# A routed encoder layer on one core: token columns of four experts made together, branches moved ahead of the gate product, a further round's products ahead of the down products

## The reference, cut to what matters

```python
# TOK = 512 tokens (two requests of 256), D = 1024, 32 experts of width 512, top 2 of 8 in the top group of 4
h = (LN(x) * (1 + scale1) + shift1)
t = token_mixer(h)                        # large dense products, done by 431 us
x = LN(alpha * x + gate1 * t)
h = (LN(x) * (1 + scale2) + shift2)
logit_g, logit_e = h @ w_router_group, h @ w_router_expert
top_logit, top_idx = top_k(logit_e of the token's best group, 2)
gate = softmax(logit_g)[g_sel] * softmax(top_logit)
for each expert e:                        # xb: the tokens that chose e
    y = (silu(xb @ w_exp_gate[e]) * (xb @ w_exp_up[e])) @ w_exp_down[e]
f = sum over a token's two experts of gate * y
x = LN(alpha * x + gate2 * f)
```

## Time and profile before

| | |
|---|---|
| median of 3 runs | 959.8 us |
| the profiled execution | 961.72 us, its span 959.9 us |
| TensorE (PE) busy | 913.3 us, 95% |
| VectorE (DVE), ScalarE (ACT), GpSimd (POOL) busy | 382.2, 244.7, 113.2 us |
| chain that ended last, by engine | PE 84%, DVE 4%, ACT 3%, issue 3%, DMA 2% |
| read from and written to HBM | 275.81 and 23.09 MB |

### The profile page before, as it was taken

The page is one execution under the profiler, slowest core; times in us unless marked ns, Lnnn a source line. Parts: engine busy times, 40 slices in busy tenths (PEclk is TensorE's granted clock), DMA queues, the critical chain, the costliest instruction groups (busy, mean ns, idle before and its releaser), DMA issues.

```text
span 959.9 us, 11508 instructions
## 1 busy us (share of the span) xinstructions
PE 913.3 (95%) x4269; PEld 538.9 (56%) x4269; DVE 382.2 (40%) x666; ACT 244.7 (25%) x357; POOL 113.2 (12%) x142
## 2 busy tenths in 40 slices
PE   3999999999999999999999999999898999999994
PEld 2567766888888888786444444434444444444331
DVE  4533443565344236788532223213222222232235
ACT  2422234432233235445411011101100110111024
POOL 2210366000001000000000000000000000000031
PEclk9999999999999999999999999999999999999997
DMA  9985654265565623809999999999999799999974
GB/s 369 348 281 175 252 220 175 88 235 202 206 233 152 178 96 120 267 0 417 375 384 427 425 426 428 426 427 427 426 429 425 315 426 426 428 427 427 423 269 136
DMA packets 47509, 295.51 MB, mean 308 GB/s; under 512 B 5046, under 2 KB 7190, under 8 KB 32082
## 3 DMA queue, kind: packets, MB, share of 16 engines
q1 hardware_dynamic: 37216, 263.99, 68.1%
q0 software_dynamic: 9616, 29.02, 9.1%
q10 hardware_dynamic: 610, 1.66, 0.5%
HBM read 275.81 MB, written 23.09 MB: 311 GB/s over the span
## 4 chain that ended last, share of the span: by engine, by line
PE 84%; DVE 4%; ACT 3%; issue 3%; DMA 2%; SPq 2%; POOL 0%; DVEq 0%; POOLq 0%; ACTq 0%
PE bank L609 81%; PE bank L893 2%; SPq L382 2%; ACT x_rows L1123 2%; DMA modraw<-in_w_mod 1%; DMA y_first<-round_y,pos_y 1%; PE bank L674 0%; DVE wo_lo L1693 0%; DMA round_y<-yout,store_row 0%; DVE y_second L2100 0%; DVE y_second L2113 0%; ACT w_hi L1123 0%; POOL y_second L597 0%; DVE bank L2108 0%; DVE yout L1988 0%
## 5 line engine op out<-in xcount | busy, mean ns | idle before, releaser
L609 PE MATMUL bank<-up_w,x_t 128*64 128x512 f32 x512 | 225.0, 592 | 0.0
L609 PE MATMUL bank<-gate_w,x_t 128*64 128x512 f32 x512 | 225.0, 592 | 0.0
L609 PEld LDWEIGHTS bank<-gate_w,x_t 128*64 128x64 f32 x512 | 70.1, 137 | 142.6 <-issue 142.6
L609 PE MATMUL bank<-h_hi,w_hi 128*128 128x512 f32 x320 | 124.8, 390 | 0.3 <-ACT h_hi L1157 0.3
L609 PE MATMUL bank<-down_w,hid_t 128*64 128x512 f32 x512 | 117.1, 598 | 8.1 <-issue 7.2
L609 PE MATMUL bank<-h_hi,w_lo 128*128 128x512 f32 x320 | 124.7, 390 | 0.0
L609 PE MATMUL bank<-h_lo,w_hi 128*128 128x512 f32 x320 | 124.5, 397 | 0.0
L1357 ACT ACTIVATE sg_hid<-bank 64x512 f32<-64x512 f32 x33 | 19.5, 592 | 350.7 <-PE bank L609 350.7
L1970 DVE TENSOR_TENSOR sg_hid<-bank,sg_hid 64x512 f32<-64x512 f32 x32 | 22.2, 694 | 201.6 <-ACT sg_hid L1357 201.5
L1528 DVE TENSOR_TENSOR w_lo<-raw,w_hi 128x1024 fp32r<-128x1024 f32 x56 | 68.5, 1225 | 77.2 <-ACT w_hi L1123 77.1
L581 POOL DMA_INDIRECT round_y<-yout,store_row x31 | 31.3, 1009 | 486.5 <-DVE yout L1988 460.2
(11 more groups left out here) (319 smaller groups left out, 1109.7 us busy)
## 6 DMA issues: line engine op xcount, KB each, us to landing
down_w<-in_w_exp_down SPq DMA_DIRECT2D x32, 2048.0 KB, 18.1
gate_w<-in_w_exp_gate SPq DMA_DIRECT2D x30, 2048.0 KB, 15.9
up_w<-in_w_exp_up SPq DMA_DIRECT2D x30, 2048.0 KB, 20.8
modraw<-in_w_mod SPq DMA_DIRECT2D x24, 1024.0 KB, 7.6
raw<-in_w_in SPq DMA_DIRECT2D x9, 2048.0 KB, 9.8
round_y<-zrow POOLq DMA_DIRECT2D x6, 2048.0 KB, 7.6
raw<-in_w_branch_b SPq DMA_DIRECT2D x2, 2048.0 KB, 9.5
raw<-in_w_branch_a SPq DMA_DIRECT2D x2, 2048.0 KB, 10.7
```

The costliest lines, as they stand in the source:

```text
L609: return pe.matmul(out, lhsT, rhs, start=start, stop=stop, skip_group_check=True)
```

## The change

There are five edits.

1. The token columns are made without rows. `chosen_group` writes a 0/1 matrix for four experts at once (`sel_group`, 256 slots by 512 tokens), once in four experts. TensorE takes the tokens `h2_hi`, `h2_lo` as the stationary operand and moves `sel_group`, so that bank 2 receives columns: 16 products of 256 columns give two of the eight chunks for four experts (`pair_begun` 12, `pair_ended` 4). ScalarE copies them (`pair_columns`). Each expert 4 to 27 makes one such pair for the next group of four, experts 2 and 3 two each, experts 28 to 31 none. The transposes of rows, the copy to `x_rows` and VectorE's copies to `x_t` are gone from expert 2 on. `x_by_expert` and `x_by_pair` are two views of one memory that alternate from group to group.
2. TensorE and ScalarE branch ahead of an expert's gate product, and no longer behind it.
3. VectorE writes `sel_x` for every expert from 2 on, ahead of its branch and of the main product `hidden` (`further_ahead`), whether the expert has a further round or not.
4. In an expert with a further round, TensorE does the further selection first, then the main gate product, then the further gate product, and both down products last.
5. In the routing, VectorE's copy of `h2_t` stands some rows earlier, and one product that keeps TensorE busy has 256 columns in place of 512.

```diff
+        next_slots = at("next_slots", [128, CAP], f32, S0 + 2048)
...
+        x_by_expert = at("x_by_expert", [128, 4, KC, CAP], f32, T0 + 24576)
+        x_by_pair = at("x_by_pair", [128, 4, 4, 2, CAP], f32, T0 + 24576)
...
+        sel_group = at("sel_group", [128, TILES, 4, CAP], f32r, T0 + 32768)
...
+        def pairs_selected(e):
+            return {2: (0, 1), 3: (2, 3)}.get(e, (e,) if 4 <= e < NEXP - 4 else ())
...
-            clock_kept(1)
+            clock_kept(256)
             logits(3)
...
+            def chunk_selected(kc, tiles):
+                for i in tiles:
+                    for piece in (h2_hi, h2_lo):
+                        x = mm(B[2][:, 256 * (kc % 2):256 * (kc % 2) + 256], piece[i][:, kc, :], sel_group[:, i, :, :].rearrange("p a s -> p (a s)"),
+                               start=(i == 0 and piece is h2_hi), stop=(i == TILES - 1 and piece is h2_lo))
+                return x
+
+            def pair_begun(n):
+                pe.wait_ge(m_sem["sl"], 4 + n // 4)
+                pe.wait_ge(m_sem["xt"], 5 + n)
+                chunk_selected(2 * (n % 4), range(TILES))
+                chunk_selected(2 * (n % 4) + 1, range(2))
+
+            def pair_ended(n):
+                chunk_selected(2 * (n % 4) + 1, range(2, TILES)).then_inc(m_sem["xs"], 1)
...
+            def expert(e):
+                if e:
+                    more = pe.value_load(tab[0:1, 0, bass.ds(e, 1)], min_val=0, max_val=7)
                 if e >= 2:
                     parted(pe, f"pe_{e}", more)
-                select_next(e)
-                residual_ahead(e)
-                main_transposes(e)
-                next_columns(e)
-                main_down(e)
+                main_gate_up(e)
+                if e < 2:
...
+                else:
+                    pairs = pairs_selected(e)
+                    for n in pairs[0:1]:
+                        pair_begun(n)
+                    residual_ahead(e)
+                    main_transposes(e)
+                    for n in pairs[0:1]:
+                        pair_ended(n)
+                    main_down(e)
+                    for n in pairs[1:]:
+                        pair_begun(n)
+                        pair_ended(n)
...
             def with_further(e):
                 more, first = turns_of(e)
-                further_selected(first)
+                further_selected(first, dve_selx, e)
+                main_gate_up(e)
+                further_columns(first)
+                for n in pairs_selected(e):
+                    pair_begun(n)
+                    pair_ended(n)
+                further_gate_up(e, first)
                 main_transposes(e)
-                further_columns(first)
                 main_down(e)
-                further_gate_up(e, first)
-                select_next(e)
                 further_transposes(first)
-                next_columns(e)
                 further_down(e, first)
...
+            def pair_columns(n):
+                act.wait_ge(m_sem["xs"], 6 + n)
+                p = n % 4
+                out = x_by_pair[:, p, :, :, :] if n // 4 % 2 == 0 else x_by_expert[:, :, 2 * p:2 * p + 2, :]
+                copy(out, B[2][:, :].rearrange("p (c a s) -> p a c s", c=2, a=4)).then_inc(m_sem["xt"], 1)
...
+            def further_ahead(e):
+                first = dve.value_load(tab[0:1, 1, bass.ds(e, 1)], min_val=0, max_val=FURTHER)
+                dve.wait_ge(x_sem["yo"], first + 1)
+                dve.wait_ge(x_st, 32 * first + 16)
+                dve.wait_ge(dve_selx, 1)
+                dve.tensor_tensor(sel_x[:, :, :, :],
+                                  next_slots[:, :].rearrange("p (i a s) -> p i a s", i=1, a=1).broadcast_to([128, TILES, 2, CAP]),
+                                  slot_of[:, e, :].rearrange("p (i a s) -> p i a s", a=1, s=1).broadcast_to([128, TILES, 2, CAP]),
+                                  ALU.is_equal).then_inc(dve_selx, 1)
...
+            def chosen_group(first):
+                dve.wait_ge(m_sem["xs"], 1 + first)
+                dve.tensor_tensor(sel_group[:, :, :, :],
...
                     if e % 3 == 0:
                         sides(e)
+                    further_ahead(e)
                     parted(dve, f"dve_{e}", more)
                     hidden(e)
                     gate_rows(e)
-                    next_chunks(e)
                     out_rows(e)
+                    next_group(e)
                     joined_again(dve, f"dve_{e}")
```

More of the change, by code:

```diff
@@ L3 @@
 from contextlib import ExitStack
+from functools import partial
 D = 1024
@@ L826, in clock_kept @@
             def clock_kept(n):
-                for _ in range(n):
-                    mm(B[7][:, :], ident, cst[:, 0:512])
+                mm(B[7][:, 0:n], ident, cst[:, 0:n])
             h2_transposes(0, (B[4], B[5]))
@@ L956, in main_down, with main_gate_up @@
                 down(hid_t, d, B[1], range(FC // 2, FC)).then_inc(m_sem["ym"], 1)
-            def expert(e, last=False):
-                s, a = e % 3, e % 2
+            def main_gate_up(e):
+                s = e % 3
                 loaded = 32 * (e // 3 + 1) + (32 if s == 0 and e >= 3 else 0)
-                if e:
-                    more = pe.value_load(tab[0:1, 0, bass.ds(e, 1)], min_val=0, max_val=7)
+                last = e == NEXP - 1
                 if e == 3:
@@ L1095, in _ @@
             expert(30)
-            expert(31, last=True)
+            expert(31)
             pe.wait_ge(act_sel, 1)
@@ L1378, in further_round, with main_silu @@
                 hid_columns(x_sem, B[7], hid_t_x, turns)
+            def main_silu(e):
+                gate_silu(m_sem, B[0], sg_hid, e, 0)
+                if e == NEXP - 1:
+                    for j, row in enumerate((ln2_g, ln2_b)):
+                        act.dma_start(ln2_bc[:, j, :], row[0, :].partition_broadcast(128)).then_inc(s_ln2, 16)
+                    act.wait_ge(pe_sel, 1)
+                    copy(last_t[:, :, :].rearrange("p i n -> p (i n)"), B[2][:, :]).then_inc(act_sel, 1)
             def with_further(e):
@@ L2024, in expert @@
                     gate_rows(e)
[L2025 to L2027 removed]
+                    for half, bank in enumerate((B[2], B[4])):
+                        dve.wait_ge(m_sem["xtr"], 4 + half)
+                        columns_in(x_by_expert[:, 2:4, 4 * half:4 * half + 4, :], bank).then_inc(m_sem["xt"], 1)
+                    chosen_group(4)
                     out_rows(e)
```

130 lines of the change are left out of this document (63 added, 67 removed).

## The result

The changed kernel takes 964.4 us in the median (962.93 to 967.04, 6 executions) beside 960.57 for the kernel before (958.33 to 961.98, 6): ratio 1.0039, with a 95% interval of 1.0024 to 1.0054. The forecast was 958.0, the range ended at 963.0, and slower had a chance of 0.17. The profiled execution took 963.12 us, with a span of 961.4.

A forecast was written before the change was run, and what follows sets the result against it. Weights and TensorE both run near their limit; behind expert 19 TensorE sets the pace at 13.83 us an expert. Terms +0.4 - 7.3 + 3.4 + 1.7 = -1.8 us, from the median 959.8 to 958.0 us; range 951.5 to 963.0.

The forecast's parts named there:

- edit 1's term: Experts 20 to 30: columns of four experts save 0.73 us in each of eight, 0.75 in two, 7.3 us in sum.
- expert 19: Expert 19's gate product to expert 20's: new order with a branch stall of 4.4 us takes 35.5 us, +0.4.
- the wait in expert 20: Expert 20's transposes: TensorE waits once for `hidden`, held up by `sel_x` and the store of expert 19's further rows, +3.4 us.
- the half clock behind it: Expert 20, after TensorE's new gap of 3.4 us: the clock drops to 0.50, +1.7 us.
- each tenth of a microsecond per expert comes off the end: Behind expert 19: TensorE sets the pace at 13.83 us an expert, so savings per expert shorten the kernel in full.
- between the two: Down products up to expert 18: waits of 2.2 us lie between 1.36 (clock kept) and 3.36 (half clock); 1.2 us left to range.
- loads in turn: Edit 1's 16 products: rival that stationary loads bind, following columns at 0.21 us each, not side by side; 966.2 us, chance 0.15.
- Edit 2's branches: Branches ahead of the gate product: 0 us, hidden by the queued down product; up to 3 us over 11 experts if not.
- as long as the weights never stop: Up to expert 18: everything saved or added, including second pairs in experts 2 and 3, only changes the wait for weights; 0 us.
- up to expert 13: Chain of the kernel before: TensorE alone sets the pace there, at 13.83 us an expert.

The follow-up runs named there:

- the first experiment: Changed kernel, but VectorE writes no `sel_x` ahead for expert 20, so it doesn't wait there for expert 19's store: 960.77 us, ratio 0.9995.
- edit 1 alone: Kernel before plus only the columns of four experts; branches, further path's order and `sel_x` as before: 961.72 us, 1.0007; with right-sized fill 959.81 us, 0.9982.
- Taking one load away: Kernel with `sel_x` laid over `x_rows_x`, without the transfer of expert 24's down weights (its rows come out wrong): 959.53 us, 0.9977.
- the trace with the fill: Changed kernel plus right-sized fill products in experts 12 to 18 and 28 to 30, wait in expert 20 kept: median 963.72 us, 1.0021; slowest execution traced.
- `sel_x` apart: Changed kernel with `sel_x` laid over `x_rows_x` instead of `yout_x`, the store wait moved to the first write of `yout_x`: 961.90 us, 1.0001.
- left out at the end: Kernel with `sel_x` laid over `x_rows_x`, fill products only in experts 12 to 18, none in 28 to 30: 961.43 us, 1.0012.
- the filled pair: Two kernels with right-sized fill: the changed kernel, 963.72 us (1.0021), and the one with `sel_x` laid over `x_rows_x`, 959.55 us (0.9977).
- the run with the branch behind: Changed kernel with TensorE's branch behind the gate product again, and in the further path the selecting products behind it: 967.18 us, 1.0058.
- Leaving out the second pairs: Changed kernel without the 32 selecting products of experts 2 and 3's second pairs (columns of experts 4 to 7 wrong): 968.29 us, 1.0058.
- with the other edits, and the branch behind: Filled kernel with `sel_x` over `x_rows_x`: 959.55 us, 0.9977; also with TensorE's branch behind the gate product and expert 19's pair before further transposes: 958.53 us, 0.9963.

## Why the prediction was wrong

**The step that failed most, in the two traces, is the size of edit 1's term.** Expert 30's down product was to start 1.8 us earlier and starts 1.47 later. Of this, down(18) is +0.6 (nothing was forecast), expert 19 +1.1 (for +0.4), the wait in expert 20 +3.1 (for +3.4), the half clock behind it +1.7 (for +1.7), and edit 1 the rest, -5.0 (for -7.3). So edit 1's term makes 2.3 of the 3.3 us. The medians lie 3.8 us apart and not 1.4; no slower execution of the changed kernel was traced, so what these lose is inferred from the experiments.

**The second step that failed** is the sentence that behind expert 19 "each tenth of a microsecond per expert comes off the end". It held for the kernel before, but not much beyond it. 6 MB an expert go out at 428 GB/s, in some 15 us, and TensorE with groups takes 13.4; without the wait in expert 20 the lead of the weights from expert 19 is used up at down(28). From there on the kernel waits for weights (0.6 us more than the gap in the first experiment, 1.3 with edit 1 alone), and drops to half clock on top, 1.4 to 1.7 us. Taking one load away gave 2.4 us back. This and the late down(18) are why edit 1 alone came out at 1.0007. In the changed kernel's own trace this step cost nothing yet: the wait in expert 20 has put TensorE back, and down(28) finds its weights there (0.47 us is its usual gap behind ScalarE's copy, below). In the trace with the fill, 966.47 us, they are late by 1.26 us in spite of the wait, which costs the transfers time too (shares of 0.94 and 0.91 at 780 to 800 us, against 1.01 and 1.00 with `sel_x` apart).

```profile
888.53 3.65 PE L624 MATMUL bank<-down_w,hid_t 128*64 128x512 f32 x16 [0.47 <-ACT hid_t L1170]
```

When the stream stopped and set out again stands in the earlier trace rows: I summed TensorE's savings and never asked how far ahead the weights were.

**The clock** was the third failure. I put the waits of 2.2 us before expert 19 "between the two" and left 1.2 us to the range. In the traces without fill every wait of 1.65 us or more ahead of a down product (from 640 us on) is followed by half clock, and of those of 1.3 to 1.6 us some are and some aren't. In experts 12 to 18 that seems to cost little, but without the pair products experts 28 and 29 have gaps of 1.51 and 0.47 us each: there half clock followed an added wait in four traces without fill, and came with no added wait in two. The fill is worth 2.3 to 2.4 us by the ratios in the two versions without the wait in expert 20 that were run with and without it, and nothing if it is left out at the end.

**Edit 1's size** was about 4.9 us, not 7.3: 0.46 us in each of eight experts and some 0.6 in two. The spacing of 0.12 was right; missing were the two first products of a series, 0.22 each, which is 0.20 of the 0.26 us an expert. The Trainium skill, TensorE: Matmul & The Clock Gate, section LDWEIGHTS, gives 107 ns for loading 128 columns. I had used it to tell loads side by side with columns (0.107) from loads in turn (0.21). Within a series the trace's 0.12 agrees with side by side; the 0.22 of its first product would fit in turn, but no run here shows that this is the reason.

**Expert 20** went as worked out: 3.06 us of wait for 3.4 and 1.69 of half clock for 1.7. That term was right, and the runs without the wait show it as the cause of the changed kernel's loss. By the ratios the same is worth 3.6 (with `sel_x` apart) to 4.2 us (the filled pair). The stream can take part of the gain away when the wait goes.

**Expert 19** took 39.7 us from down(18) to expert 20's gate product, 1.1 more than before, for +0.4 forecast; the stall was 4.70 for 4.4, and expert 22's gate weights went out at 757.92 us, 0.8 earlier and not 2. That `sel_x` isn't what TensorE waits for there, but its own branch, is shown by the run with the branch behind.

**Edit 2's branches** cost nothing visible where no further round is due: 13.37 with them ahead and with them behind. **Before expert 19** the forecast put every change at nothing, "as long as the weights never stop". They do stop for moments at experts 2 and 3 (share 0.93 at 510 to 520 us, where 1.02 stood). In the traces of the kernels with groups down(18) starts between 726.6 and 729.5 us, mostly later than the 726.8 of the kernel before. Leaving out the second pairs didn't bring it back (728.7), and with the fill it stands anywhere between 726.6 and 728.9, so the cause stays open. The chain also shows the first wait for weights at expert 13 already (0.84 us), where the forecast had TensorE alone "up to expert 13".

**The ledger of the medians:** +3.8 us in all. The wait in expert 20 is 3.6 to 4.2 of it, so without it the changed kernel equals the one before. Once the wait is gone, the groups' 4.9 us come through as nothing while the last experts run into weights and half clock. With the fill they come through as 1.7 us (0.9982, edit 1 alone; the interval is 0.4 to 3.0); with the other edits, and the branch behind, it is 2.2 and 3.6 (0.9977, 0.9963).

## What to carry to other kernels

When a slower engine hides a stream of transfers behind it, work out how long the stream's lead lasts at the new, shorter period before you count the saving for every iteration: here it lasted eight of eleven experts. Where a short gap of TensorE has lost the work that filled it, a fill product of the gap's own length, measured first, can bring back what the wait and the lower clock took. And before you write a buffer ahead of time, look at whose memory it lies on: another address took the whole wait away.

## What the runs showed of the hardware that was not expected

- The kernel with `sel_x` laid apart spreads over 8 us, in step with its mean granted clock: 957.87 us at 0.991, 965.61 us at 0.981. The kernel before spreads nearly as far (958.6 to 965.65) at 0.988 to 0.996, so the clock isn't all of it. One profiled execution can't stand for the median.
- TensorE's wait of 1.76 us at 680 us was followed by a stretch at half clock, the kernel before's waits of 1.4 us weren't; with groups, waits of 1.31 and 1.40 us were in two traces, and one of 1.60 us wasn't. In experts 28 to 30 gaps of 1.50 and 0.47 us with four transposes between them came before half clock in two executions and not in others.
- An f32 product of 512 columns took 0.885 us with 128 rows and some 0.44 with 64, in two passes each.
- The time from the end of what VectorE does to the first instruction behind its branch was 5.79 us when the branch is taken, TensorE's stall 3.1 to 5.3, depending on what is queued ahead.
